# Feed-forward stages of a hybrid diffusion step: the first two pairs by plain products, weight blocks made load by load, groups placed 1-1-1-1-6

## The chip, the cores and the metric

The kernel runs on one core of one Trainium2 chip. The time is device microseconds (us) of one execution; lower is better. The engines are TensorE (PE; its weight loads are PEld), VectorE (DVE), ScalarE (ACT), GpSimd (POOL) and SyncE (SP), which here only issues DMAs.

## The reference

One step through two trunk layers for 640 tokens of 1024 features: 128 context tokens (tile 0) and 512 latent tokens (tiles 1 to 4). Layer 0 mixes with a gated MLP and a bidirectional recurrence, layer 1 with windowed attention. Each layer ends in the stage that the change is about:

```python
hp = modulate(rmsnorm(xp, norm_ffn_pre[layer]), mod_p[3], mod_p[4])
hs = modulate(rmsnorm(xs, norm_ffn_pre[layer]), mod_s[3], mod_s[4])
xp = xp + mod_p[5] * rmsnorm(sq_relu_mlp(hp, w_ffn_in[layer], w_ffn_out[layer]), norm_ffn_post[layer])
# sq_relu_mlp(h, w1, w2) = square(relu(h @ w1)) @ w2;   w1: 1024 x 4096, w2: 4096 x 1024;   xs likewise
```

Everything is in fp32. The modulation parameters (`silu(c) @ w_mod + b_mod`) of later places are computed beside other stages, 1 MB of `w_mod` at a time.

## The kernel before, in words

**Precision.** Each fp32 operand is cut into a high part (rounded to the matmul's input type by ScalarE: a "cast") and a low part (the rest: one subtraction on GpSimd or VectorE). A product of two operands is three matmuls (`split3`, L1917 to L1919): high by high, and the two mixed ones.

**Pairs.** The 4096 hidden features are worked through in 16 pairs of 2 x 128. A pair's first product is a 2 x 2 block product: weights A11, A12, A21 (its place is taken by S1), A22 of 512 features x 128 outputs each, inputs B11, B12, B21, B22 of 512 features x 320 tokens. The kernel makes it by Strassen's method in Winograd's form: 7 products P1 to P7 instead of 8, of 12 matmuls with 320 columns each. For it VectorE makes S1 to S4 of the weights in place (`adds`, L1526 to L1533) and, once per stage, T1 to T4 of the inputs (`comb`, in three slices of columns: 64, 128, 128); ScalarE casts each and GpSimd makes the low half (L1481 for the weights, L1460 for the inputs). VectorE joins the seven results (L1724 to L1733), ScalarE squares and casts them (`squared`), VectorE takes the low half (`rests`, L1541) into FH/FL.

**Groups.** The second product of a pair is 10 groups (5 token tiles x 2 output halves) of 6 matmuls with 512 columns. A group goes into one of two PSUM banks in turn; VectorE adds it to ACC (L1830) and so gives the bank back. The last two pairs are done together in G2, one step per token tile.

**Weights.** A pair's w1 and w2 are 1 MB each and are loaded by SP into RAW, which has two places: one is w1's, the other w2's. A load waits until the low halves of all blocks of the one before it in its place are made. The blocks (units of 512 columns) go to a ring of 12. For each stage an order of units is written out, and a small planner gives each unit the earliest step ("event") at which ScalarE is to cast it: after the unit 12 places before it was last used, 3 events after the last block of the load before in its place. S1 to S4 are added one event before their cast.

**Order.** All engines go through one list of steps, each in order. In the steady part pair p+1's products are interleaved with pair p's groups: P1, P6, P2, 2 groups, P5, 2 groups, P7, 2, P4, 2, P3, 2. In layer 0 the modulation of pairs 0 to 6 stands behind the second group and its transposes behind the fifth. At the head of a stage the last tiles are still being normed and transposed (`T_`, `turned_rows`, `cut`), and the order is: transposes of tile 2, P1 of pair 0, transposes of tile 3, P1 of pair 1, transposes of tile 4, P2 of pair 0, modulation, P2 of pair 1, then P6, P5, P7, P4, P3 of pair 0, then pair 1's with pair 0's groups. Before T2 and T4 overwrite X, X is stored to DRAM (`x_out`).

## Time and profile before

| | us |
|---|---|
| median of 3 runs | 1532.7 (1532.35 to 1532.74) |
| the profiled execution, its own time | 1531.43 |
| its span | 1529.6 |
| TensorE busy | 1388.7 (91%) |
| VectorE / ScalarE / GpSimd busy | 960.9 / 713.9 / 735.6 |
| mean granted TensorE clock, share of full | 0.972 |

A busy TensorE is not TensorE at its peak: matmuls overlap, so the spacing of their starts is what counts, and idle time is read from the waits. The layers' feed-forward stages are about 258 to 757 us and 1033 to 1529 us of the span.

### The profile page before, as it was taken

The numbers are of one execution on the slowest core, as the hardware profiler recorded it, in microseconds if no ns is written. First come the engines' busy times: TensorE is split into PE (matmuls) and PEld (weight loads), VectorE is DVE, ScalarE is ACT, GpSimd is POOL, SyncE is SP. The second block draws the span as 40 slices with busy tenths as digits, with TensorE's granted clock in tenths as the row PEclk, the third lists the DMA queues.
The fourth block names the chain that finished last, engine by engine and source line by source line (L and its number), as shares of the span: only waits on it lengthen the run. The fifth ranks groups of instructions, "written<-read, shape, count | busy, mean of one in ns | idle before, by whom it ended". The sixth has DMA issues, their size and how long they took to land.

```text
span 1529.6 us, 20862 instructions
## 1 busy us (share of the span) xinstructions
PE 1388.7 (91%) x7634; PEld 1163.8 (76%) x7634; DVE 960.9 (63%) x1577; ACT 713.9 (47%) x1444; POOL 735.6 (48%) x559
## 2 busy tenths in 40 slices
PE   5999997699899999999999999994899999999998
PEld 3877876577788888888867867783788888888886
DVE  5477837664466566575664588457665665766656
ACT  4467625443344344344551467555443443443443
POOL 1331413664455455455342578435564554555550
PEclk9999999799999999999999999997999999999999
DMA  9434252344543211312455100123313113122123
GB/s 351 136 109 139 84 196 82 131 157 127 184 157 111 97 69 56 110 56 83 151 192 172 55 1 2 47 64 124 138 65 128 57 56 111 56 67 99 56 83 138
DMA packets 97916, 164.33 MB, mean 107 GB/s; under 512 B 11084, under 2 KB 49688, under 8 KB 97816
## 3 DMA queue, kind: packets, MB, share of 16 engines
q1 hardware_dynamic: 86176, 157.23, 30.1%
q10 hardware_dynamic: 11640, 5.76, 1.5%
q8 instruction: 63, 1.03, 0.3%
q14 instruction: 37, 0.30, 0.1%
HBM read 154.82 MB, written 8.16 MB: 107 GB/s over the span
## 4 chain that ended last, share of the span: by engine, by line
PE 38%; DVE 4%; issue 3%; POOL 2%; ACT 2%; DMA 2%; SPq 0%; DVEq 0%; ACTq 0%; POOLq 0%
PE PS L1917 11%; PE PS L1918 10%; PE PS L1919 10%; PE PS L2253 1%; PE PS L2242 1%; PE PS L2221 1%; POOL WLU L1481 1%; DMA xd<-X 1%; PE PS L2222 1%; PE PS L1967 1%; PE PS L2205 1%; DVE X L1641 0%; DMA RAW<-in_w_ffn_in 0%; POOL GG L1428 0%; PE PS L2198 0%
## 5 line engine op out<-in xcount | busy, mean ns | idle before, releaser
L1481 POOL TENSOR_TENSOR WLU<-RAW,WHU 128x512 fp32r<-128x512 f32 x352 | 483.7, 1396 | 440.7 <-ACT WHU L1148 440.7
L1148 ACT CAST WHU<-RAW 128x512 fp32r<-128x512 f32 x352 | 204.7, 617 | 231.6 <-DMA RAW<-in_w_ffn_in 127.2
L1917 PE MATMUL PS<-WHU,MXR 128*128 128x512 f32 x640 | 257.5, 402 | 51.8 <-issue 41.5
L1830 DVE TENSOR_TENSOR ACC<-ACC,PS 128x512 f32<-128x512 f32 x260 | 175.2, 682 | 137.0 <-PE PS L1919 135.9
L1918 PE MATMUL PS<-WLU,MXR 128*128 128x512 f32 x640 | 252.4, 394 | 0.0
L1919 PE MATMUL PS<-WHU,MXR 128*128 128x512 f32 x640 | 251.6, 393 | 0.0
L1476 POOL TENSOR_TENSOR WL<-RAW,WH 128x512 fp32r<-128x512 f32 x84 | 117.5, 1430 | 213.3 <-ACT WH L1139 195.8
L1917 PEld LDWEIGHTS PS<-WHU,MXR 128*128 128x128 f32 x640 | 121.2, 189 | 90.2 <-issue 61.9
L1917 PE MATMUL PS<-HH,WHU 128*128 128x320 f32 x512 | 161.0, 314 | 20.6 <-DVE HL L1680 14.9
L1919 PE MATMUL PS<-HH,WLU 128*128 128x320 f32 x512 | 159.5, 311 | 0.0
L1918 PE MATMUL PS<-HL,WHU 128*128 128x320 f32 x512 | 159.3, 311 | 0.0
L1919 PEld LDWEIGHTS PS<-WHU,MXR 128*128 128x128 f32 x640 | 121.2, 189 | 26.8
L1918 PEld LDWEIGHTS PS<-WLU,MXR 128*128 128x128 f32 x640 | 121.4, 190 | 19.0
L1541 DVE TENSOR_TENSOR MXR<-MX,MXR 128x320 fp32r<-128x320 f32 x128 | 131.5, 1030 | 2.6 <-ACT MXR L1186 2.6
L1917 PEld LDWEIGHTS PS<-HH,WHU 128*128 128x128 f32 x512 | 97.4, 190 | 31.4 <-DVE HL L1680 15.4
L1184 ACT ACTIVATE MX<-MX 128x320 f32<-128x320 f32 x96 | 45.3, 472 | 162.5 <-DVE MX L1728 66.3
L1917 PE MATMUL PS<-WH,HH 128*128 128x512 f32 x280 | 112.6, 402 | 1.5 <-DVE ACC L1837 0.7
L1919 PE MATMUL PS<-WH,HL 128*128 128x512 f32 x280 | 109.3, 390 | 0.0
L1918 PE MATMUL PS<-WL,HH 128*128 128x512 f32 x280 | 109.1, 390 | 0.0
L1918 PEld LDWEIGHTS PS<-HL,WHU 128*128 128x128 f32 x512 | 97.4, 190 | 3.0
L1917 PE MATMUL PS<-XT,WHU 128*128 128x320 f32 x256 | 80.7, 315 | 19.9 <-POOL HFR L1460 19.9
L1919 PEld LDWEIGHTS PS<-HH,WLU 128*128 128x128 f32 x512 | 97.3, 190 | 0.0
(265 smaller groups left out, 2763.6 us busy)
## 6 DMA issues: line engine op xcount, KB each, us to landing
RAW<-in_w_ffn_in SPq DMA_DIRECT2D x32, 1024.0 KB, 6.7
RAW<-in_w_ffn_out SPq DMA_DIRECT2D x32, 1024.0 KB, 8.8
RAW<-in_w_mod SPq DMA_DIRECT2D x18, 1024.0 KB, 5.6
GG<-in_w_mod SPq DMA_DIRECT2D x13, 1024.0 KB, 9.4
MX<-in_w_mod SPq DMA_DIRECT2D x11, 1024.0 KB, 7.6
RAW<-in_w_in_even SPq DMA_DIRECT2D x7, 1024.0 KB, 5.4
RAW<-in_w_qkv SPq DMA_DIRECT2D x6, 1024.0 KB, 6.7
xd<-X SPq DMA_DIRECT2D x10, 512.0 KB, 10.3
```

The costliest lines, as they stand in the source:

```text
L1148: nc.scalar.copy(unit_view(WHU, u), unit_raw(u["ld"], u["of"])).then_inc(u_hi, 1)
L1184: link(nc.scalar.activation(z, z, ACT.Relu))
L1476: ins = nc.gpsimd.tensor_tensor(cut(ring_view(WL, ld, j)), cut(w_view(ld, b)), cut(ring_view(WH, ld, j)).bitcast(f32), ALU.subtract)
L1481: nc.gpsimd.tensor_tensor(unit_view(WLU, u), unit_raw(u["ld"], u["of"]), unit_view(WHU, u).bitcast(f32), ALU.subtract)\
L1541: V_.tensor_tensor(FL[:, slot, cols], FZ[:, slot, cols], FH[:, slot, cols].bitcast(f32), ALU.subtract).then_inc(ff_lo, 1)
L1830: V_.tensor_tensor(acc, acc, PS[:, 4 + b % 2, :], ALU.add).then_inc(b_free[b % 2], 1)
L1917: MM(out, wh, xh, start=first, stop=False, skip_group_check=reopens)
L1918: MM(out, wh, xl, start=False, stop=False, skip_group_check=reopens)
L1919: return MM(out, wl, xh, start=False, stop=last, skip_group_check=reopens)
L1967: ins = MM(PS[32 * kt:32 * kt + 32, 6 + u % 2, :], CL[:, 4 * kh + kt, :], rv[:, kt, :], start=(kh == 0), stop=(kh == 1))
L2205: ins = TR(m_bank(u)[:, P * h:P * h + P], Q2[s["n"] % 2][:, P * h:P * h + P], IDN[:, :])
L2221: MM(out, q, KH[:, g, keys], start=True, stop=False)
```

## The change

In words:
- Pairs 0 and 1 of each stage are made without the Winograd form: for each of two output blocks f and each of two column ranges (tokens 0 to 255, and 256 to 639) one step `N` of 8 x 3 matmuls, straight from the plain input. They need only A11, A12, A21, A22, so eight units and no S. ScalarE squares each result directly from its bank.
- The head's order is: transposes of tile 2, norm of tile 4, N of (pair 0, f 0, early columns), transposes of tile 3, N(0,1,early), transposes of tile 4, N(1,0,early), N(1,1,early), then the four late ones with the slices of `comb` between them, the modulation, T1 for all columns (`comb1`), and pair 0's ten groups in one run. T2 is now made from T3, and T1 is left out of the slices.
- From pair 2 on the products are Winograd's as before, with 1 group behind P6, P2, P7 and P4 and 6 behind P3; modulation behind the third group, its transposes behind the seventh.
- The order of units is now load by load (seven of w1, then four of w2); a unit may be cast 6 events (4 in the head) after the last block of the load before in its place. w2 of a pair is asked for just before w1 of the pair after the next.

```diff
@@ def ffn: order of steps
-        product(0, "P1")
-        T_(ph, TT - 2, cut=False, groups=True)
+        asked = fill[0] + (mod_load(*fill.pop(0)),)
+        w2_load(0)
         step("norm", ph=ph, t=TT - 1)
-        cut_()
+        direct(0, 0, 0)
+        T_(ph, TT - 2, groups=True)
+        direct(0, 1, 0)
+        T_(ph, TT - 1, groups=True)
+        direct(1, 0, 0)
+        direct(1, 1, 0)
         step("comb", layer=layer, c=0)
-        product(1, "P1")
+        direct(0, 0, 1)
         step("comb", layer=layer, c=1)
-        T_(ph, TT - 1, groups=True)
-        product(0, "P2")
-        mod(*fill.pop(0))
-        w2_load(0)
+        direct(0, 1, 1)
         step("comb", layer=layer, c=2)
-        product(1, "P2")
-        step("comblo", layer=layer)
-        flush()
-        for name in ("P6", "P5", "P7", "P4", "P3"):
-            product(0, name)
-        for p in range(PAIRS - 2):
+        w1_load(2)
+        direct(1, 0, 1)
+        direct(1, 1, 1)
+        mod(*asked)
+        step("comb1", layer=layer)
+        for q in range(2 * TT):
+            group(0, q)
+            if q == 4:
+                flush()
+        for p in range(1, PAIRS - 2):
             asked = fill[0] + (mod_load(*fill.pop(0)),) if fill else None
+            w2_load(p)
             w1_load(p + 2)
-            w2_load(p + 1)
             q = 0
-            for name, ngroups in ((("P6", 0), ("P5", 2), ("P7", 3), ("P4", 3), ("P3", 2)) if p == 0 else
-                                  (("P1", 0), ("P6", 0), ("P2", 2), ("P5", 2), ("P7", 2), ("P4", 2), ("P3", 2))):
+            for name, ngroups in (("P1", 0), ("P6", 1), ("P2", 1), ("P5", 0), ("P7", 1), ("P4", 1), ("P3", 6)):
...
-                    if q == 2 and asked:
+                    if q == 3 and asked:
                         mod(*asked)
-                    elif q == 5:
+                    elif q == 7:
                         flush()
@@ def ffn: order and place of the units
-        order = [(0, "A11"), (0, "A12"), (1, "A11"), (1, "A12"), (0, "S2"), (0, "S1"), (0, "A22"), (0, "S4"), (0, "S3"),
-                 (1, "S2"), (1, "S1"), (1, "A22"), (0, 0, 0), (0, 1, 0), (1, "S4"), (1, "S3"), (0, 0, 1), (0, 1, 1)]
+        order = [(p, name) for p in (0, 1) for name in ("A11", "A12", "A21", "A22")] + [(0, kt, nh) for nh in (0, 1) for kt in (0, 1)]
         for p in range(2, PAIRS):
...
-            order += [(p, "A11"), (p, "A12"), (p, "S2"), w2[0], w2[1], (p, "S1"), (p, "A22"), (p, "S4"), w2[2], w2[3], (p, "S3")]
+            order += [(p, name) for name in ("A11", "A12", "S2", "S1", "A22", "S4", "S3")]
+            if p < PAIRS - 1:
+                order += [(p - 1, kt, nh) for nh in (0, 1) for kt in (0, 1)]
...
-                    at = max(at, max(place[x] for x in place if of_load(x) == ring_order[r - 2]) + 3)
-                if o[-1] in ("S2", "S3", "S4") and o[0] > 1:
+                    freed = max(place[x] for x in place if of_load(x) == ring_order[r - 2])
+                    at = max(at, freed + (4 if freed < NS else 6))
+                if o[-1] in ("S4", "S3"):
+                    cycle = NS + 2 * TT + 17 * (o[0] - 3)
+                    at = max(at, cycle + 9 if o[0] > 2 else NS + 1)
@@ VectorE
                 elif k == "g":
                     b, acc = s["b"], ACC[:, s["t"], 512 * s["nh"]:512 * s["nh"] + 512]
                     upto(dve, b_ready, b)
+                    if not s["p"]:
+                        dve.wait_ge(t_add, 12 * s["layer"] + 12)
@@ TensorE
+                elif k == "N":
+                    layer, p, f, part = s["layer"], s["p"], s["f"], s["part"]
...
+                    if part:
+                        pe.wait_ge(n_read, DIRECTS[layer, p, f, 0])
+                    if p == 0 and f == 0:
+                        for half in (0, 1):
+                            pe.wait_ge(f_lo[half], TT * layer + (2, 5)[part])
+                    out = direct_bank(s)
+                    for i in (0, 1):
+                        u = s["units"][i]
+                        pe.wait_ge(u_lo, u["number"] + 1)
+                        wh, wl = unit_view(WHU, u), unit_view(WLU, u)
+                        for kt in range(4):
+                            xh, xl = HH[:, 4 * i + kt, DIRECT[part]], HL[:, 4 * i + kt, DIRECT[part]]
+                            ins = split3(out, (wh[:, kt, :], wl[:, kt, :]), (xh, xl), (i, kt) == (0, 0), (i, kt) == (1, 3))
+                    ins.then_inc(n_done, 1)
```

With this order, in a steady pair: A11 to A22 of pair p+2 are cast behind P1, P6, P2, the second group and P5 of pair p+1; S1 is added at P6, S2 behind the first group, S4 at P4, S3 behind the fourth group and cast behind P3; w2's four blocks are cast behind the fifth, sixth, seventh and tenth groups.

## Rows read from the trace of the kernel before

**Rows 1.** The page's first part: engine, busy us, share of the span, instructions.
```profile
PE 1388.7 (91%) x7634; PEld 1163.8 (76%) x7634; DVE 960.9 (63%) x1577; ACT 713.9 (47%) x1444; POOL 735.6 (48%) x559
```
**Rows 2.** Waits of TensorE, whole span: waiting line, releaser, total us, times, longest.
```profile
PE PS L1917 <- issue: 41.5, 28, 6.0
```
**Rows 3.** By stage: us; busy PE, PEld, DVE, ACT, POOL (count); clock; DMA share; GB/s.
```profile
258.50:338.00 79.50, 53.17 (x292) 44.82 (x293) 55.29 (x78) 40.19 (x88) 46.81 (x35) 0.83 0.43 152
338.00:720.40 382.40, 362.50 (x1994) 313.67 (x1993) 232.77 (x322) 156.86 (x314) 198.73 (x145) 0.99 0.31 102
1033.40:1112.80 79.40, 53.11 (x293) 44.71 (x294) 55.47 (x78) 40.26 (x88) 46.83 (x35) 0.83 0.36 126
1112.80:1481.10 368.30, 346.12 (x1873) 306.83 (x1872) 232.62 (x300) 156.77 (x313) 198.85 (x145) 1.00 0.24 78
```
**Rows 4.** Timeline, TensorE, head of layer 0: start, us, instruction, [idle before].
```profile
258.52 0.30 PE L2007 MATMUL PS<-IDN,ACC 128*128 128x128 f32 x1 [0.63 <-DVE ACC L1671]
267.03 0.64 PE L1917 MATMUL PS<-HH,WHU 128*128 128x320 f32 x1 [7.45 <-DVE HL L1680]
296.73 0.61 PE L1917 MATMUL PS<-XT,WHU 128*128 128x320 f32 x1 [9.87 <-POOL HFR L1460]
312.07 0.47 PE L1917 MATMUL PS<-WHU,MXR 128*128 128x512 f32 x1 [1.52 <-POOL WLU L1481]
```
**Rows 5.** Timeline, TensorE and VectorE, steady part of layer 1.
```profile
1212.15 0.69 DVE L1526 TENSOR_TENSOR RAW<-RAW 128x512 f32<-128x512 f32 x1 [3.70 <-DMA RAW<-in_w_ffn_in]
1212.76 0.68 DVE L1830 TENSOR_TENSOR ACC<-ACC,PS 128x512 f32<-128x512 f32 x1
1213.54 0.47 PE L1917 MATMUL PS<-WHU,MXR 128*128 128x512 f32 x1 [1.32 <-issue]
```
**Rows 6.** Timeline, TensorE: half a modulation step; firsts of P1, P6, two groups, P5.
```profile
317.29 1.07 PE L1967 MATMUL PS<-MX,CL 128*32 128x512 f32 x8
...
1112.79 0.30 PE L1917 MATMUL PS<-HH,WHU 128*128 128x320 f32 x1
1114.55 0.31 PE L1917 MATMUL PS<-XT,WHU 128*128 128x320 f32 x1
...
1118.07 0.39 PE L1917 MATMUL PS<-WHU,MXR 128*128 128x512 f32 x1
...
1120.81 0.30 PE L1917 MATMUL PS<-HH,WHU 128*128 128x320 f32 x1
```
**Rows 7.** Timeline, TensorE, mixer of layer 0: firsts of 24 matmuls each.
```profile
53.91 0.28 PE L1917 MATMUL PS<-HH,WH 128*128 128x256 f32 x1
...
56.79 0.34 PE L1917 MATMUL PS<-HH,WH 128*128 128x384 f32 x1
...
60.98 0.28 PE L1917 MATMUL PS<-HH,WH 128*128 128x256 f32 x1
```
**Rows 8.** Timeline, VectorE, ahead of the stage of layer 0.
```profile
253.82 1.58 DVE L1526 TENSOR_TENSOR RAW<-RAW 128x512 f32<-128x512 f32 x1
255.32 1.77 DVE L1531 TENSOR_TENSOR RAW<-RAW 128x512 f32<-128x512 f32 x1
```
**Rows 9.** Loads: a wait for X's stores, one w1 load's issue and use, w1's median (page: KB each, us to landing).
```profile
275.88 0.43 DVE L1702 TENSOR_TENSOR XTF<-ACC,EARLY_H 128x256 f32<-128x256 f32 x1 [1.83 <-DMA xd<-X]
374.97 0.37 SPq L1092 DMA_DIRECT2D RAW<-in_w_ffn_in  x1
388.17 0.62 ACT L1148 CAST WHU<-RAW 128x512 fp32r<-128x512 f32 x1 [11.05 <-DMA RAW<-in_w_ffn_in]
RAW<-in_w_ffn_in SPq DMA_DIRECT2D x32, 1024.0 KB, 6.7
```
**Rows 10.** Groups by line: VectorE from 1184 to 1436 us, and GpSimd's cut (page): count, busy us, mean ns.
```profile
L1541 DVE TENSOR_TENSOR MXR<-MX,MXR 128x320 fp32r<-128x320 f32 x36 | 43.1, 1197 | 0.0
L1533 DVE TENSOR_TENSOR RAW<-RAW 128x512 f32<-128x512 f32 x18 | 22.2, 1235 | 0.0
L1481 POOL TENSOR_TENSOR WLU<-RAW,WHU 128x512 fp32r<-128x512 f32 x352 | 483.7, 1396 | 440.7 <-ACT WHU L1148 440.7
```

More of the change, by code:

```diff
@@ L257, in ffn, with holder @@
                         for nh in (0, 1):
-                            used[p, kt, nh] = e
-        place, before = {}, -2
-        ring_order = [x for p in range(PAIRS) for x in ([("w1", p)] + ([("w2", p - 1)] if p else []))] + [("w2", PAIRS - 1)]
+                            uses((p, kt, nh), e)
+        def holder(k):
+            return k - UNITS + (2 if k < 2 * UNITS - 2 else 0)
+        place, before = {}, -3
         ring_order = [("w1", 0), ("w1", 1)] + [x for p in range(PAIRS - 2) for x in (("w2", p), ("w1", p + 2))] + \
@@ L297, in ffn @@
                     steps[events[e + late]].setdefault("rest", []).append((s["p"], s["name"]))
+            elif s["kind"] == "N":
+                s["units"] = [by_name[layer, s["p"], f"A{s['f'] + 1}{k}"] for k in (1, 2)]
+                steps[events[e + 1]].setdefault("rest", []).append((s["p"], (s["f"], s["part"])))
             elif s["kind"] == "g":
@@ L841, in hybrid_step @@
         GROUP_B = {(s["layer"], s["p"]): s["b"] for s in STEPS if s["kind"] == "g"}
-        RESTS = {(s["layer"], s["p"], s["name"]): k + 1 for k, s in
-                 enumerate(s for s in STEPS if s["kind"] == "P" and s["name"] in OUTPUT)}
+        RESTS = {}
+        for s in STEPS:
+            if s["kind"] == "N" or s["kind"] == "P" and s["name"] in OUTPUT:
+                RESTS[s["layer"], s["p"], s["name"] if s["kind"] == "P" else (s["f"], s["part"])] = len(RESTS) + 1
         TURNS = {(s["ph"], s["t"]): s for s in STEPS if s["kind"] == "T"}
@@ L953, in ring_view @@
             return buf[:, j % RING, :]
+        DIRECTS = {(s["layer"], s["p"], s["f"], s["part"]): i + 1 for i, s in enumerate(s for s in STEPS if s["kind"] == "N")}
         BLOCK_LOAD = {}
@@ L1022, in out_cols, with bank_of, direct_bank, outputs_done @@
             return slice(HALF * late, HALF * late + HALF)
-        def bank_of(name, p):
-            b = {"P1": 2 if p == 1 else 0, "P2": 2 if p == 1 else 0, "P6": 1, "P7": 1, "P5": 2, "P3": 2, "P4": 3}[name]
-            return PS[:, b, 0:HALF]
+        def bank_of(name):
+            return PS[:, {"P1": 0, "P2": 0, "P6": 1, "P7": 1, "P5": 2, "P3": 2, "P4": 3}[name], 0:HALF]
+        DIRECT = (slice(0, 2 * P), slice(2 * P, TOK))
+        NP = PAIRS - 2
+        def direct_bank(s):
+            cols = DIRECT[s["part"]]
+            return PS[:, 2 * s["p"] + s["f"], 0:cols.stop - cols.start]
+        def outputs_done(layer, p, t):
+            return RESTS[layer, p, ("P4" if t < 2 else "P3") if p > 1 else (1, int(t > 1))]
+        def output(slot, name):
+            if name in OUTPUT:
+                f, late = OUTPUT[name]
+                return slot + f, out_cols(late)
+            return slot + name[0], DIRECT[name[1]]
         def modc(layer, c):
@@ L1720, in _ @@
                         dve.wait_ge(p_done, s["count"] + 1)
[L1721 removed]
+                        bank = bank_of(name)
                     if name == "P6":
```

202 lines of the change are left out of this document (102 added, 100 removed).

## The prediction

> **What bounds the kernel now.** I read the page's busy times first: TensorE is busy for 91% of the span, no other engine for more than 63% [rows 1]. So time can only be won where TensorE stands still or does work that can be left out. The list of its waits says where: 41.5 us in 28 waits are put down to "issue" [rows 2], none of them to a named engine. The busy table by stage then splits each feed-forward stage in two [rows 3]. In the head (from the transposes of tile 2 to the first product of pair 2; 79.5 and 79.4 us) TensorE is busy for 53 us only and its mean clock is 0.83; in the rest up to the first product of pair 15 (382.4 and 368.3 us) it is busy 94 to 95%.
>
> The head's timeline shows the holes [rows 4]: 7.45 us before the first product (it needs the low half of tile 2), 9.87 us before P6 (it needs T2 of all columns), 1.52 us before the first second-matrix group (its block's low half is late). Between them products and transposes wait for one another, and after a hole the granted clock is at the lower of its two levels (1.2 of 2.4 GHz) for a while, hence the mean of 0.83 [rows 3].
>
> In the steady part one hole comes back in each pair: 1.32 us before the matmul at 1213.54. The profile calls it "issue", but VectorE's rows at the same moment name it [rows 5]: VectorE stood 3.70 us in front of S1 (L1526), waiting for the load of w1, and the accumulation of a group (L1830, 1212.76 to 1213.44) is queued behind it. TensorE waits for that bank and goes on 0.1 us after it ends. The accumulation itself was due long before.
>
> **Prices.** A product (12 matmuls of 320 columns) takes 1114.55-1112.79 = 1.76 us, two groups (12 matmuls of 512 columns) 1120.81-1118.07 = 2.74 us, so 1.37 each [rows 6]. A pair without holes is 7 x 1.76 + 10 x 1.37 = 26.0 us. The 13 pairs between the bounds of the steady part [rows 3] would be 338.0 us. Layer 1 takes 368.3 [rows 3], 30.3 more, 2.3 per pair; layer 0 382.4, of which six modulation steps are 13.3, leaving 31.1: a step is 16 matmuls of which eight last 1.07 us [rows 6], so 1.9 with overlap, and four transposes, 0.3; 2.2 in all.
>
> **Part 1, plain products in place of the first two pairs.** Each pair now has four results (two output blocks by 256 and 384 columns) of 24 matmuls each. The same shapes stand in an earlier stage: 24 of 256 columns take 56.79-53.91 = 2.88 us, 24 of 384 take 60.98-56.79 = 4.19 [rows 7]. Four and four are 28.3 us, against 14 products at 1.76 = 24.6: TensorE has 3.7 us more work per layer. What goes for it:
> - Nothing in the first four results needs tiles 2 to 4. They need tiles 0 and 1, both halves of the features. Tile 1's low half stood behind two additions on VectorE (1.58 and 1.77 us [rows 8]) that pairs 0 and 1 no longer need; without them it ends at about 258.4, and the first result starts at about 259, right behind the transposes of tile 2, which start at 258.52 [rows 4]. The 7.45 us go.
> - The four early results (11.5 us) lie beside the norm, transposes and cuts of tiles 3 and 4. Tile 4's transposes must wait until VectorE has read tile 3's bank: I count about 1 us of waiting there. Tile 4's low half is there at about 273, when the four have ended: 0.3 us.
> - The four late ones (16.8 us, about 273.5 to 290) lie beside the three T2, T3, T4 combinations, which therefore stop nothing; the 9.87 us and the wait ahead of them go. T1 shares its place with the plain input, so it comes behind the last plain result, but its first user (P5 of pair 2) is over 15 us later.
> - The second-matrix blocks of pair 0 are cut beside them, so the 1.52 us go.
>
> TensorE's own sum for the head is then 0.8 (transposes of tile 2) + 28.3 + 1.6 (two more tiles' transposes) + 2.2 (modulation) + 13.7 (ten groups) = 46.7 us. VectorE becomes the second limit: of the 55 us it had here [rows 3] I take off 14 of combinations, low halves and additions of pairs 0 and 1 and add 3 for low halves of tiles 3 and 4: some 44 us, with gaps. In order on it stand the modulation copy, the three T1 additions (about 3 us) and only then the first copies out of the groups' two banks, then S4 and S3 of pair 2. ScalarE has a wait of its own: the casts of w2 of pair 0 stand behind the third plain result (at about 272), and that load comes behind five 512 KB stores of X, whose wait ended at 275.88 in the profile [rows 9]; ScalarE will stand until about 278 with the squares behind it, and VectorE's low halves wait for those. I put 9 us on the sum for all this: 55.5 us in place of 79.45. Its bounds are 49 (the waits of 1 and 0.3 and 1 at the groups) and 68 (the store's landing and T1's chain both in full, 6 and 8 us, and the lower clock behind them for 4). Gain 24 us per layer, 48 in all.
>
> The first modulation after the head falls one pair later, so one of them (2.2 us) moves from each head into the steady part.
>
> **Part 2, blocks load by load, and groups 1-1-1-1-6.** Before, w1's last block (S3) and w2's last blocks were cut together, and the next w1 was asked for only then, 6.7 us (the page's median to landing [rows 9]) ahead of VectorE's first need. Now w1's seven blocks come first. I count in one pair from the start of P1: P4 ends at 14.7, P3 at 17.8, six groups end at 26.0, and the next P1 and P6 at 29.5. S3 is cast behind P3's squares, its low half ends at about 22.3; 6.7 us later, at 29.0, w1 is there, and VectorE comes to S1 behind P6, at 30.1. So nothing waits, and what would be late next has room: behind S1 stands only the accumulation of one group, whose bank TensorE needs again 6.6 us later, since P2, a group, P5 and P7 lie between. Even the longest landing that I found (asked for at 374.97, used at 388.17, 13.2 us [rows 9]) would not quite reach it. The w2 load is asked for at about 28 and first needed at 47. In layer 0 the two modulation loads go out just ahead of w2 at about 15 and the three land by 25 to 28; w2's casts are due at 22 and the groups that use them at 31.7: covered.
>
> What can be late is VectorE in the six groups. From the end of P4 (t = 0) it has c21 0.5, S4, the low half of P7, one accumulation 0.7, S3, c12 0.5, the low half of P4, and then the accumulation of group 4. TensorE needs that bank at 5.9. A low half takes 1.20 on average and an addition like S3 1.24 [rows 10]; the accumulation (L1830) reads PSUM and is not changed by its neighbours. With these means: 0.5+1.2+1.2+0.7+1.2+0.5+1.2+0.7 = 7.2, late by 1.3. With the short values (0.7 for the additions, 0.5 for the low halves) 4.8, not late. GpSimd has nothing to cut during the first half of that stretch, so I take a value between: 1.0 us per pair, from 0 to 3.
>
> The Trainium skill ("SBUF — State Buffer", section "Who interferes with whom") says that a VectorE instruction with two SBUF inputs and a GpSimd instruction that reads SBUF exclude each other for a whole instruction. The trace agrees: L1541 (two inputs in SBUF) has a mean of 1.20 us [rows 10], and the accumulation, which reads one input from PSUM, takes 0.68 [rows 5]. Rival D is what the rule would do at its worst.
>
> So a steady pair is 27.0 us. Layer 0: 13 x 27.0 + 7 x 2.2 = 366.4, against 382.4, 16.0 less. Layer 1: 351.0 + 2.2 = 353.2 against 368.3, 15.1 less. The tail behind pair 15's first product keeps its order and its wait, and I leave it at nothing, as everything outside the feed-forward stages: its instructions don't change.
>
> **Sum.** 48 + 16 + 15 = 79 us off the profiled execution's 1531.4 us (span 1529.6): 1452.4. The median of the runs is 1.3 us above that execution, so I forecast 1454 us.
>
> **Rivals.**
> - A, TensorE's floor: the head at 51 and a pair at 26.2 us. For it: in the trace TensorE keeps 26.0 whenever nobody holds it. Heads 57 less, steady part 26 + 26 less: 1422. 12%.
> - B, the six groups stall on VectorE: 3.0 us per pair, the four two-input operations at the length that they have beside GpSimd (1.5 to 1.7, as the additions of [rows 8]). Against it: GpSimd is busy for half of the time only. That is 26 x 2.0 = 52 us more than forecast: 1506. Half of that (2.0 per pair): 1480. Together 20%.
> - C, the head gives back: w2's late load and T1's chain leave it at 68 us. 2 x 12.5 more: 1479. 8%.
> - D, slower than before: the six-group run again, but with each of the four two-input operations first waiting for a whole cut of GpSimd (mean 1.40 [rows 10]) and then running (0.5 to 0.7), and GpSimd's cuts delayed by them in turn, so that the next pair's blocks are late too. It decides from 79/26 = 3.0 us per pair above my 1.0, so from 4.0; at 4.5 the time is 1454 + 26 x 3.5 = 1545. In full that is 4 x 2.0 + 2.4 = 10.4 (four of them lie ahead of the bank) against 5.9 available, 4.5 late. Against it: GpSimd has some two cuts in that stretch, not four. 4%.
> - E, the holes have another cause (instruction supply, as "issue" could be read) and stay, and the head's are eaten by the added products: about no change, 1532. The 0.1 us between accumulation and restart [rows 5] speaks against it. 2%.
> The forecast has the remaining 54%, with a range of its own of 1438 to 1470. For 8 in 10 the range takes in part of A, C and half of B: 1430 to 1488. A change of 0.2% is about what a measurement of this kernel can tell: faster 94%, within 0.2% 2%, slower 4%.
>
> **What would show it.** The head of each layer (transposes of tile 2 to P1 of pair 2) at 52 to 60 us, with a granted clock near 1 and no wait of TensorE over 2 us until the groups. In the steady part 26.2 to 28 us per pair, no VectorE wait for w1 with an accumulation due behind it, and what is left of waiting inside the last six groups, behind accumulations. Wrong would be: a head over 65 us, a wait of TensorE for a combination or a block's low half in pair 2, or pairs at 28 us and more.

## The result and the profile after

The changed kernel takes 1441.1 us (median of 4 runs, 1440.0 to 1441.7) against 1532.7 us: ratio 0.940, 95% interval 0.9385 to 0.9417, so 92 us less. The forecast was 1454 (1430 to 1488). The profiled execution has a span of 1439.6 us, 90.0 less than before.

The page's first part, as in [rows 1], and TensorE's waits, as in [rows 2]:

```profile
PE 1373.5 (95%) x7682; PEld 1163.8 (81%) x7682; DVE 853.0 (59%) x1541; ACT 705.3 (49%) x1428; POOL 718.3 (50%) x547
```

```profile
PE PS L1970 <- issue: 17.1, 4, 8.3
```

The table by stage, with the same bounds and columns as [rows 3] (transposes of tile 2, first product of pair 2, first product of pair 15, in layer 0 and in layer 1):

```profile
258.80:320.60 61.80, 50.81 (x297) 45.08 (x296) 48.05 (x60) 34.71 (x77) 42.90 (x30) 0.92 0.51 179
320.60:676.80 356.20, 356.20 (x2014) 311.43 (x2013) 191.08 (x325) 156.30 (x313) 194.62 (x144) 1.00 0.35 116
988.74:1051.20 62.46, 51.12 (x297) 45.23 (x296) 48.11 (x60) 34.68 (x77) 42.92 (x30) 0.92 0.50 177
1051.20:1392.50 341.30, 341.22 (x1894) 306.85 (x1894) 184.42 (x303) 155.66 (x313) 195.96 (x144) 1.00 0.26 84
```

In the steady part nothing is left to win by removing waits: TensorE is busy in all of it, at the full clock. The heads still have waits. Against [rows 3] the heads give 17.6 and 16.8 us, the steady parts 26.3 and 27.0, and the tail 1.4 (48.5 to 47.1; its wait before P2 is gone); the sum is 89.1, and most of the rest of the 90.0 lies between the stages (from the first product of pair 15 of layer 0 to the head of layer 1, 313.1 to 311.9).

The 26.3 us of layer 0's steady part don't come evenly from its 13 pairs. One of them (pair 3, from its first product to pair 4's) took 37.3 us and now takes 28.6. In the kernel before, VectorE stood there 10.41 us for w1 and TensorE 5.97 us behind it (timelines):

```profile
388.18 0.69 DVE L1526 TENSOR_TENSOR RAW<-RAW 128x512 f32<-128x512 f32 x1 [10.41 <-DMA RAW<-in_w_ffn_in]
389.57 0.76 PE L1917 MATMUL PS<-WHU,MXR 128*128 128x512 f32 x1 [5.97 <-issue]
```

This is the load of [rows 9] that landed 13.2 us after it was asked for. It was asked for 3.5 us behind a store of the new state (4 KB), which ScalarE issues together with three other transfers (two of 256 KB, one of 4 KB). In the kernel after, the w1 load nearest to that store goes out 6.3 us ahead of it and lands in 5.4 us. The 14 traces of this case divide in this way: the w1 load nearest to the store lands in 5.4 to 5.7 us where it is asked for ahead of it (nine traces), and in 11.7 to 15.2 us where it is asked for 0.4 to 3.5 us behind it (five). No run separates the four transfers. So 8.7 us of layer 0's gain go with the place of one load.

TensorE in the head of layer 0 (timeline; start, duration, instruction, wait before it), the answer to [rows 4]:

```profile
258.81 1.04 PE L2060 MATMUL PS<-IDN,ACC 128*128 128x128 f32 x8
...
267.65 0.63 PE L2060 MATMUL PS<-IDN,ACC 128*128 128x128 f32 x4 [1.06 <-DVE ACC L1730]
269.87 1.12 PE L2060 MATMUL PS<-IDN,ACC 128*128 128x128 f32 x4 [1.59 <-ACT ACC L1213]
...
306.87 0.77 PE L1970 MATMUL PS<-WHU,MXR 128*128 128x512 f32 x1 [7.87 <-issue]
...
316.48 0.47 PE L1970 MATMUL PS<-WHU,MXR 128*128 128x512 f32 x1 [0.47 <-issue]
```

The 7.45, 9.87 and 1.52 us of [rows 4] are gone. In their place stands one hole of 7.87 us ahead of the third group (8.29 in layer 1). As in [rows 5], the word "issue" hides a bank that VectorE has not read yet. In the kernel before this holds for every one of the 28 waits of [rows 2]: each ends 0.10 us after VectorE's accumulation or copy out of a bank has ended. Behind a wait for w1 stood 22 of these, behind a wait for GpSimd's cut four, and the other two are in the heads. VectorE at that moment, and what ScalarE waited for earlier (timelines):

```profile
296.43 1.70 DVE L1591 TENSOR_TENSOR RAW<-RAW 128x512 f32<-128x512 f32 x1 [1.25 <-POOL WLU L1541]
298.05 3.18 DVE L1600 TENSOR_TENSOR MXR<-MX,MXR 128x384 fp32r<-128x384 f32 x2
301.16 0.68 DVE L1645 COPY PART<-PS 128x512 f32<-128x512 f32 x1
301.76 4.21 DVE L1764 TENSOR_TENSOR EARLY_H<-ACC 128x256 f32<-128x256 f32 x3
306.07 0.69 DVE L1885 COPY ACC<-PS 128x512 f32<-128x512 f32 x1
```

```profile
279.87 1.14 ACT L1202 CAST WHU<-RAW 128x512 fp32r<-128x512 f32 x2 [3.22 <-DMA RAW<-in_w_ffn_out]
```

Read upwards from the copy (L1885) that frees the first group's bank: three T1 additions (L1764), the modulation copy (L1645), two low halves of plain results (L1600), S2 (L1591). Groups 1 and 2 had filled both banks by 299.0; TensorE goes on 0.11 us after the copy ends.

In the steady part of layer 1, VectorE around the last six groups of a pair:

```profile
1173.14 0.49 DVE L1781 TENSOR_TENSOR MX<-PS,MX 128x320 f32<-128x320 f32 x1 [1.06 <-PE PS L1972]
1173.55 0.68 DVE L1593 TENSOR_TENSOR RAW<-RAW 128x512 f32<-128x512 f32 x1
1174.15 0.48 DVE L1600 TENSOR_TENSOR MXR<-MX,MXR 128x320 fp32r<-128x320 f32 x1
1174.55 0.68 DVE L1883 TENSOR_TENSOR ACC<-ACC,PS 128x512 f32<-128x512 f32 x1
1175.15 0.68 DVE L1593 TENSOR_TENSOR RAW<-RAW 128x512 f32<-128x512 f32 x1
1176.29 0.49 DVE L1784 TENSOR_TENSOR MX<-PS,MX 128x320 f32<-128x320 f32 x1 [0.45 <-PE PS L1972]
1176.69 0.68 DVE L1600 TENSOR_TENSOR MXR<-MX,MXR 128x320 fp32r<-128x320 f32 x1
1177.67 0.69 DVE L1883 TENSOR_TENSOR ACC<-ACC,PS 128x512 f32<-128x512 f32 x1 [0.29 <-PE PS L1972]
```

These are the very operations that the forecast summed. VectorE waits for TensorE among them (1.06, 0.45, 0.29), not the other way round. GpSimd's cuts (timeline) leave a gap of 4.50 us there, from 1171.24 to 1175.74:

```profile
1167.13 4.11 POOL L1541 TENSOR_TENSOR WLU<-RAW,WHU 128x512 fp32r<-128x512 f32 x3 [2.90 <-ACT WHU L1202]
1175.74 1.29 POOL L1541 TENSOR_TENSOR WLU<-RAW,WHU 128x512 fp32r<-128x512 f32 x1 [4.50 <-ACT WHU L1202]
```

### The profile page after: what moved, and what is told of

The parts are those of the page before. It is cut to its first block and busy times, and to the rows that moved or that the text cites. A ratio compares the mean times of both kernels' runs of the same rounds, so it can differ in the third digit from the quotient of the medians.

```text
span 1439.6 us, 20860 instructions
## 1 busy us (share of the span) xinstructions
PE 1373.5 (95%) x7682; PEld 1163.8 (81%) x7682; DVE 853.0 (59%) x1541; ACT 705.3 (49%) x1428; POOL 718.3 (50%) x547
## 5 line engine op out<-in xcount | busy, mean ns | idle before, releaser
L1541 POOL TENSOR_TENSOR WLU<-RAW,WHU 128x512 fp32r<-128x512 f32 x340 | 460.5, 1378 | 371.2 <-ACT WHU L1202 371.2
L1202 ACT CAST WHU<-RAW 128x512 fp32r<-128x512 f32 x340 | 195.7, 618 | 161.4 <-PE PS L1972 117.8
L1970 PE MATMUL PS<-WHU,MXR 128*128 128x512 f32 x640 | 253.6, 396 | 19.4 <-issue 17.1
L1970 PE MATMUL PS<-HH,WHU 128*128 128x320 f32 (+2 forms) x576 | 178.9, 311 | 0.0
L1972 PE MATMUL PS<-HH,WLU 128*128 128x320 f32 (+2 forms) x576 | 178.7, 310 | 0.0
L1971 PE MATMUL PS<-HL,WHU 128*128 128x320 f32 (+2 forms) x576 | 178.7, 310 | 0.0
L1972 PEld LDWEIGHTS PS<-WHU,MXR 128*128 128x128 f32 x640 | 121.0, 189 | 26.6
L1970 PEld LDWEIGHTS PS<-HH,WHU 128*128 128x128 f32 x576 | 109.5, 190 | 4.9 <-issue 0.2
L1971 PEld LDWEIGHTS PS<-HL,WHU 128*128 128x128 f32 x576 | 109.4, 190 | 4.3
L1972 PEld LDWEIGHTS PS<-HH,WLU 128*128 128x128 f32 x576 | 109.3, 190 | 0.0
L1600 DVE TENSOR_TENSOR MXR<-MX,MXR 128x320 fp32r<-128x320 f32 (+2 forms) x128 | 89.3, 702 | 8.5 <-ACT MXR L1322 7.2
L1970 PE MATMUL PS<-XT,WHU 128*128 128x320 f32 x224 | 70.0, 312 | 0.0
```

What stands on the lines that cost most here:

```text
L1202: nc.scalar.copy(unit_view(WHU, u), unit_raw(u["ld"], u["of"])).then_inc(u_hi, 1)
L1541: nc.gpsimd.tensor_tensor(unit_view(WLU, u), unit_raw(u["ld"], u["of"]), unit_view(WHU, u).bitcast(f32), ALU.subtract)\
L1600: V_.tensor_tensor(FL[:, slot, cols], FZ[:, slot, cols], FH[:, slot, cols].bitcast(f32), ALU.subtract).then_inc(ff_lo, 1)
L1970: MM(out, wh, xh, start=first, stop=False, skip_group_check=reopens)
L1971: MM(out, wh, xl, start=False, stop=False, skip_group_check=reopens)
L1972: return MM(out, wl, xh, start=False, stop=last, skip_group_check=reopens)
```

## The experiments

Stages in us (layer 0 / layer 1), all from profiled executions with the bounds of [rows 3]; "late pair" is the distance between first products of later pairs of layer 1; "won" is one less the ratio to before, times 1532.7, with its interval. The kernels are told of one by one below.

```
                 heads          steady parts     late pair   won
before           79.5 / 79.3    382.4 / 368.3    28.0         -
after            61.9 / 62.5    356.1 / 341.2    26.03       91.8 (89.4 to 94.3)
b_both           78.7 / 80.6    363.2 / 350.3    26.03       43.1 (40.2 to 45.8)
b_units_new      78.9 / 78.4    368.0 / 352.8    26.6        34.0 (31.6 to 36.5)
b_groups_new     80.0 / 79.5    375.5 / 361.6    27.3        15.5 (12.4 to 18.4)
b_s1_later       80.5 / 79.4    380.0 / 371.6    28.2         0.5 (-2.6 to 3.7)
a_head_only      62.4 / 62.0    378.2 / 366.0    28.1        43.4 (40.3 to 46.6)
after_again      64.0 / 63.2    356.1 / 341.2    26.03       93.0 (90.7 to 95.2)
a_w2_later       61.0 / 60.7    356.1 / 341.3    26.03       97.2 (94.1 to 100.1)
a_s12_later      58.6 / 58.1    356.8 / 342.5    26.03       99.5 (96.9 to 102.1)
a_both           57.8 / 56.7    356.7 / 342.5    26.03      103.6 (100.7 to 106.5)
a_t1_between     57.0 / 57.4    358.9 / 343.7    26.03       98.6 (96.1 to 100.9)
a_t1_early       59.5 / 58.7    358.0 / 343.5    26.03       97.2 (94.4 to 99.9)
a_pool_twice     61.6 / 62.4    356.7 / 341.2    26.03       93.0 (90.3 to 95.9)
```

### The steady part alone, in whole and in halves

The kernel before with this edit to the groups (b_groups_new), this to the order of the blocks (b_units_new), and both (b_both; there S1 is also added behind A12, as in the kernel after):

```diff
-    (("P1", 0), ("P6", 0), ("P2", 2), ("P5", 2), ("P7", 2), ("P4", 2), ("P3", 2))
+    (("P1", 0), ("P6", 1), ("P2", 1), ("P5", 0), ("P7", 1), ("P4", 1), ("P3", 6))
```

```diff
-            order += [(p, "A11"), (p, "A12"), (p, "S2"), w2[0], w2[1], (p, "S1"), (p, "A22"), (p, "S4"), w2[2], w2[3], (p, "S3")]
+            order += [(p, name) for name in ("A11", "A12", "S2", "S1", "A22", "S4", "S3")]
+            if p < PAIRS - 1:
+                order += [(p - 1, kt, nh) for nh in (0, 1) for kt in (0, 1)]
```

> The kernel before with the steady part of the change alone: blocks made load by load (w1's seven, then w2's four) and groups behind the products 1-1-1-1-6; both heads as before, the first two pairs of each stage in seven products. Theory (the trace of after read by stages): the steady part gives 53 us of the 92, the head 35 to 39, and the two do not touch each other: about 1478 us (1474 to 1483), and no TensorE start more than 0.5 us late in the steady part. Rival (the forecast's own split, head 48, steady part 31): 1501 us. Second rival: the steady part is clean only because the new head hands over an early schedule; then under 20 us are gained here, over 1512 us.

> The kernel before with one edit: a pair's blocks are made load by load (w1's seven first, then w2's four), so the next w1 is asked for as soon as S3 is cast. The groups stay where they were (none behind P6, two behind P2, P5, P7, P4, P3 and so on) and the heads too. Theory: the hole per pair is VectorE's wait for w1 ahead of S1 with an accumulation queued behind it; asking earlier takes it away by itself, and what is left is nothing: 1478 to 1485 us. Rival (the order of the groups does the work, because an accumulation must not be due close behind S1): 1510 to 1533 us, little gained. Rival (the hole is instruction supply at a fixed place in the code): 1530 us.

> The kernel before with one edit: the ten groups of a pair lie 1-1-1-1-6 behind P6, P2, P7, P4 and the last product P3, none elsewhere. The blocks are still made with w1's and w2's mixed, so w1 is asked for as late as before. Theory: VectorE still stands before S1 until w1 lands, but now with one accumulation behind it and not two, and the six groups at the end end later: between 10 and 30 us gained, 1503 to 1523 us. Rival (the groups are what the change is worth in the steady part): 1478 to 1485 us. Rival (six groups in a row stall on VectorE, the forecast's case B): 1540 us and more.

Measured: 1489.5, 1499.3 and 1517.4 us. A late pair falls from 28.0 to 27.3 by the groups, to 26.6 by the blocks and to 26.03 by both: 0.7 and 1.4 make 2.0, so in the settled pairs the two parts nearly add. The groups came out inside the theory's 1503 to 1523; the other two missed theirs by some 6 and 14 us at the slow end. Against TensorE's own time (26.03 us a pair, 28.57 with a modulation) the steady parts of b_units_new are 29 us too long. Some 10 of these are 0.6 us in each of the 17 late pairs, in which TensorE still waits 0.2 to 0.8 us for an accumulation that stands behind S2, and S2 behind GpSimd's cut. Another 8 are pair 3 of layer 0, which takes 36.8 us: its w1 was asked for 0.4 us behind the store and landed in 15.2 us, and TensorE stood 6.27 us. The rest lies in the first pairs. What b_both lacks is in its pair 2: from P1 of pair 2 to P1 of pair 3 it takes 35.5 and 38.0 us, against 28.6 and 28.9 in the kernel after. There TensorE waits in layer 1 (timeline) for a low half and behind VectorE, whose S4 had stood 3.38 us for GpSimd:

```profile
1100.88 0.47 PE L1920 MATMUL PS<-WHU,MXR 128*128 128x512 f32 x1 [3.48 <-POOL WLU L1484]
```

```profile
1120.41 1.66 DVE L1536 TENSOR_TENSOR RAW<-RAW 128x512 f32<-128x512 f32 x1 [3.38 <-POOL WLU L1484]
```

The old head hands its blocks over too late for the new order; one pair later that is over. So the second rival (clean only because of the new head) fails: 37 us of the steady part's 53 come without it, and the other 16 are the two pairs 2 (6.9 + 9.1).

### One addition moved in VectorE's queue

```diff
+                if o[-1] == "S2" and o[0] > 2:
+                    at = max(at, place[o[0], "A12"] + 2)
...
-            elif o[-1] == "A11":
+            elif o[-1] == ("A11" if o[0] < 3 else "A12"):
                 steps[index(place[o])].setdefault("add", []).append(dict(layer=layer, ld=u["ld"], of=(o[0], "S1")))
```

S1 of pairs 3 and later moves one step back, and S2 stays behind it.

> The kernel before with one addition moved on VectorE: from pair 3 on, S1 = A11+A12 stands one step later in its queue, behind A12's cut instead of behind A11's, and S2 behind that; loads, products and groups are as before, and so w1 lands as late as before. Theory (the hole is VectorE's queue: it stands for w1 in front of S1 with the accumulation that TensorE needs queued behind): the accumulation now goes ahead of the wait, and most of the 1.3 to 1.7 us per pair goes: 26 x 1.5 = 39, about 1494 us (1485 to 1505). Rival (instruction supply or whatever else the word issue covers): the time stays at 1533 us within 2. Rival (the late blocks themselves would stop TensorE next): under 15 us gained, and a wait of a product for its block in the profile.

Measured: 1532.6 us, nothing won. That is the rival's time, but not its mechanism. VectorE and TensorE in one pair (timelines):

```profile
1212.10 0.69 DVE L1528 TENSOR_TENSOR RAW<-RAW 128x512 f32<-128x512 f32 x1 [2.31 <-DMA RAW<-in_w_ffn_in]
1212.71 0.49 DVE L1543 TENSOR_TENSOR MXR<-MX,MXR 128x320 fp32r<-128x320 f32 x1
1214.44 1.69 DVE L1533 TENSOR_TENSOR RAW<-RAW 128x512 f32<-128x512 f32 x1 [1.25 <-POOL WLU L1483]
1216.06 1.27 DVE L1832 TENSOR_TENSOR ACC<-ACC,PS 128x512 f32<-128x512 f32 x2
```

```profile
1216.84 0.47 PE L1919 MATMUL PS<-WHU,MXR 128*128 128x512 f32 x1 [1.51 <-issue]
```

The wait for w1 now has no accumulation behind it, and the hole has left its place between the groups behind P5: it stands behind P7. But S2, which comes next, waits 1.25 us for GpSimd's cut and takes 1.69 us beside the next one, and two accumulations are behind that. TensorE starts 0.1 us after the first of them ends, as in [rows 5]. So my theory was right about the queue and wrong about the price: with w1 as late as before, what is made from it is late, and taking one waiting instruction out of the queue brings the next one to its front. Fixed code as the cause is refuted by the hole's move.

The same is seen from the other side in b_units_new, where VectorE still stands 3.00 us for w1 ahead of S1, but early enough for the accumulation behind it (timeline):

```profile
1244.43 0.69 DVE L1527 TENSOR_TENSOR RAW<-RAW 128x512 f32<-128x512 f32 x1 [3.00 <-DMA RAW<-in_w_ffn_in]
1245.04 0.68 DVE L1831 TENSOR_TENSOR ACC<-ACC,PS 128x512 f32<-128x512 f32 x1
```

### The head alone

The kernel before with the new head (first two pairs by plain products, in the order of the kernel after); from pair 2 on blocks and groups as before.

```diff
-            for name, ngroups in (("P1", 0), ("P6", 1), ("P2", 1), ("P5", 0), ("P7", 1), ("P4", 1), ("P3", 6)):
+            for name, ngroups in (("P1", 0), ("P6", 0), ("P2", 2), ("P5", 2), ("P7", 2), ("P4", 2), ("P3", 2)):
```

(shown against the kernel after; the order of the blocks goes back as well.)

> The kernel before with the head of the change alone: pairs 0 and 1 of each stage by plain products, in the order of the kernel after; from pair 2 on blocks mixed and groups placed as before. Theory: the head gives 35 to 40 us here as in the kernel after, and the steady part keeps its holes: 1533 - 37 = 1496 us (1490 to 1502). Rival (the forecast's sizes): 48 us, 1485 us. Rival (the two parts need each other; in the old order the head's lateness on VectorE and in the loads is carried on through the pairs): 1505 us or more.

Measured: 1491.7 us, 43.4 won (40.3 to 46.6), more than the 35 to 40 expected. The heads account for 17.1 and 17.3; another 4.2 and 2.3 lie in the first pairs of the old steady part, and its holes stay (28.1 per pair). In layer 0 the late w1 only changes its pair: 37.5 us in pair 4, with TensorE standing 6.76 us. The two parts alone make 86.5 of the whole's 91.8. The missing 5 are about what the three intervals allow. The stages show that the new order loses 10 us where it meets the old head, in b_both's pairs 2 (35.5 and 38.0, before 32.2 and 31.4), and that the new head helps the old order's first pairs.

### What makes the hole in the new head

Edits to the kernel after. a_w2_later: w2's casts of pair 0 on ScalarE one plain result later. a_s12_later: S1 and S2 of pair 2 behind T1 in VectorE's queue. a_both: both.

```diff
+                if k == 8:
+                    at = 3
+                if o == (2, "S2"):
+                    at = NS + 3
...
-                steps[index(place[o])].setdefault("add", []).append(dict(layer=layer, ld=u["ld"], of=(o[0], "S1")))
+                steps[index(place[o] if o[0] > 2 else NS + 1)].setdefault("add", []).append(dict(layer=layer, ld=u["ld"], of=(o[0], "S1")))
```

> The kernel after with ScalarE's casts of w2 of pair 0 one plain result later in each layer, so that ScalarE does not stand before them for the load while squares that VectorE needs are queued behind. Theory (the hole of 8 us between the second and third group is VectorE's queue in the head, and ScalarE's stand for the load at 276.7 to 279.9 is the first 3 us of it): 2 x 3 = 6 us less, 1435 us (1433 to 1438), and the hole at about 5 us. Rival (VectorE's own queue is full from the end of the second plain result on, and the stand only takes what would be waited for later): 1441 within 1. Rival (w2's cut now ends too late and its first group waits): 1443 us or more.

> The kernel after with the additions S1 and S2 of pair 2 moved on VectorE from ahead of the T1 additions to behind them (their first user, P1's neighbours of pair 2, comes after all ten groups). Theory: TensorE's hole of 8 us is VectorE's queue ahead of the first copy out of a group's bank; two additions (some 1.2 to 1.5 us each) less in it shorten the hole by 2.5 to 3 us per layer; the groups' run has room for them: 1435 to 1437 us. Rival (they come back as a wait between groups or of S4's product): 1441 within 1, with a smaller hole and a new one behind it.

> Both edits to the kernel after: w2's casts of pair 0 one result later, and S1, S2 of pair 2 behind T1. Theory: the two shorten the same queue and add: hole about 2 us in place of 8, 1441 - 12 = 1429 us (1428 to 1433), and more of the head at the full clock. Rival (the queue is bound by GpSimd's or ScalarE's chain once two pieces are out): 1434 to 1437 us. Rival (given back at P1 or P2 of pair 2): 1439 to 1441 us.

In a_w2_later only the first two lines (`k == 8`) are changed, in a_s12_later only the others.

Measured: 1437.6, 1435.7 and 1431.9 us. TensorE ahead of the third group of layer 0 in the three (timelines), against 7.87 in the kernel after:

```profile
304.74 0.77 PE L1972 MATMUL PS<-WHU,MXR 128*128 128x512 f32 x1 [6.94 <-issue]
```

```profile
303.75 0.47 PE L1972 MATMUL PS<-WHU,MXR 128*128 128x512 f32 x1 [4.44 <-issue]
```

```profile
302.69 0.47 PE L1974 MATMUL PS<-WHU,MXR 128*128 128x512 f32 x1 [3.56 <-issue]
```

S1 and S2 behave as the theory says: the hole is 3.4 us shorter (4.3 in layer 1, 8.29 to 3.95), with 0.6 and 1.2 us given back in the first steady pair. ScalarE's stand is worth less than I thought, 0.9 and 1.3 us of hole and not 3: VectorE's queue has more in front than what ScalarE delays. Its time fell inside the expected 1433 to 1438 us all the same, but the stages show only 2.6 us of it in the two heads, and its interval (0.9347 to 0.9386) overlaps that of the kernel after when measured again, so of this edit alone no gain is shown. The same kernel's heads differ by 2.2 and 0.7 us between two executions (after and after_again), and single holes by 1.0 us. The two edits shorten the same queue and nearly add (5.4 and 7.7 us by the ratios, 11.8 together). a_both is the fastest kernel here: its interval, 0.9305 to 0.9343 of before, lies below both of the kernel after's, 0.9385 to 0.9417 and 0.9379 to 0.9408 (after_again).

### T1 between the copies

T1's additions read only the half of the rows that the five groups with nh=0 overwrite. a_t1_between takes pair 0's groups with nh=1 first, puts one T1 addition behind each of the first three copies and S1, S2 behind the fourth (with w2's casts later, as above). a_t1_early puts S1 and S2 behind the third copy, and the small gate operations three groups later.

```diff
-            step("g", uses_b=1, layer=layer, p=p, nh=q // TT, t=q % TT)
+            step("g", uses_b=1, layer=layer, p=p, nh=q // TT if p else 1 - q // TT, t=q % TT)
...
-        step("comb1", layer=layer)
         for q in range(2 * TT):
             group(0, q)
+            for c in (0, 1, 2):
+                if q == (0, 1, 2)[c]:
+                    step("comb1", layer=layer, c=c)
...
-                        dve.wait_ge(t_add, 12 * s["layer"] + 12)
+                        dve.wait_ge(t_add, 12 * s["layer"] + (9 if s["nh"] else 12))
```

> The kernel after, unchanged, as the control for the edits to its head, in one set of runs with the next two. Both theories: 1441 us within 2, the hole between its second and third group at 7 to 8.5 us in both layers, 26.03 us per pair in the steady part of layer 1.

> The kernel after with w2's casts of pair 0 one result later, and with the T1 additions no longer ahead of the groups: pair 0's five groups of the output's second half come first (T1 reads the first half of the rows that a group's first copy overwrites, and only that), and T1's three additions lie between their copies, one behind each of the first three; S1, S2 of pair 2 behind the fourth. Theory (the hole is the 4.9 us of T1's additions, queued on VectorE ahead of the first copy out of a bank): no wait over 1.5 us at the groups, head at 55 to 57 us, 1425 us (1421 to 1430). Rival (VectorE is full all through the groups, since its additions take 1 to 1.6 us beside GpSimd's cuts and the copies 0.7, against 1.37 per group): the wait is only spread over groups three to seven, the head stays at 58 us, as with S1 and S2 alone moved: 1430 to 1434 us. Rival (given back, because T1's and w2's blocks of pair 1 come later and stop pair 2): 1436 us or more.

> The kernel a_t1_between (T1's three additions between the first group copies) with two things put back or moved: S1, S2 of pair 2 and all blocks behind them one step earlier (as in a_both), and the small gate operations of VectorE, which took 3.3 us between two copies there, three groups later. Theory (in a_t1_between the 5 us won in each head came back in part as 2.3 us at the gate operations and 2.4 us in pair 2's groups, both from VectorE's queue): both go for the most part, heads 55 to 56 us, pair 2 at 26.5 us (layer 1 with modulation 29), 1426 us (1422 to 1430), below both kernels and below a_both. Rival (VectorE is simply full through the ten groups, whatever the order): the same 57 us and 1431 to 1436 us. Rival (its queue is now worse ahead of the fourth copy): a wait of 2 us and more there, 1434 us or more.

Measured: 1441.5, 1435.8 and 1437.5 us. The hole of 7.9 us is gone in both (0.61 us in its place in layer 0, 1.41 and 1.32 in layer 1). Both kernels also have the two edits before, which had left 3.56 and 2.85 us of it. So moving T1 took away the last 3.0 and 1.5 us. S1 and S2 alone had taken 3.4 and 4.3 us, ScalarE's stand alone 0.9 and 1.3. The hole is the sum of what stands in the queue and has no single cause. But a smaller hole comes later. In a_t1_between it is 2.32 us behind two gate operations of VectorE on 128x8 elements, in a_t1_early 3.76 us behind S3, ahead of the tenth group. VectorE and GpSimd in a_t1_between, then VectorE in a_t1_early (timelines):

```profile
305.14 2.10 DVE L1665 TENSOR_TENSOR GC<-GC,GCB 128x8 f32<-128x8 f32 x1
307.28 1.19 DVE L1666 TENSOR_TENSOR GC<-GC,GCN 128x8 f32<-128x8 f32 x1
308.39 1.27 DVE L1891 COPY ACC<-PS 128x512 f32<-128x512 f32 x2
```

```profile
303.86 3.36 POOL L1527 TENSOR_TENSOR HL<-EARLY_H,HH 128x1280 fp32r<-128x1280 f32 x1 [3.13 <-ACT HH L1320]
307.18 5.46 POOL L1547 TENSOR_TENSOR WLU<-RAW,WHU 128x512 fp32r<-128x512 f32 x4
```

```profile
313.28 1.66 DVE L1599 TENSOR_TENSOR RAW<-RAW 128x512 f32<-128x512 f32 x1 [3.12 <-POOL WLU L1547]
...
315.68 0.17 DVE L1665 TENSOR_TENSOR GC<-GC,GCB 128x8 f32<-128x8 f32 x1
```

The first gate operation took 2.10 us, until GpSimd's T1 low half ended (303.86 + 3.36 = 307.22). Moved away from it, it takes 0.17 us again, but S3's addition waits 3.12 us for GpSimd's cuts, which stand behind that same T1 low half in GpSimd's queue (306.06 to 309.02 there). So neither theory was right: VectorE is not full, and the order did not cure it; the chain through GpSimd is next. Pair 2 also gives back time: in layer 1 31.35 us against 28.92. I had put that down to the blocks' coming a step later, but in a_t1_early, where they are back in their place, it still takes 31.12, and its cause stays open. Both times lie some 11 us above the theories, by the rivals in which the gain is given back. a_both, with no edit to T1, stays ahead of both, by 4 and 6 us.

### GpSimd's work doubled in the steady part

```diff
                     pool.wait_ge(u_hi, u["number"] + 1)
+                    if len(u["of"]) == 2 and u["of"][0] > 2 and u["of"][1] in ("S1", "A22", "S4", "S3"):
+                        again[0] += 1
+                        nc.gpsimd.tensor_tensor(unit_view(WLU, u), unit_raw(u["ld"], u["of"]), unit_view(WHU, u).bitcast(f32), ALU.subtract).then_inc(twice, 1)
+                        pool.wait_ge(twice, again[0])
```

> The kernel after, in which GpSimd makes the low halves of S1, A22, S4 and S3 twice in every pair from 3 on (the same values; some 5 us more of GpSimd per pair, in the stretch in which VectorE has its S4, S3 and low halves to make ahead of the six groups' accumulations). Theory (the steady part keeps TensorE's own 26.03 us per pair because GpSimd stands still in that stretch, so that VectorE's two-input operations take 0.5 to 0.7 us and not the 1.2 that the forecast reckoned with): their mean rises to 1.0 us and more, TensorE waits inside the six groups, 26.5 to 28 us per pair, 1455 to 1490 us. Rival (VectorE has room there in any case, and the forecast's order of the accumulations was wrong): VectorE's operations get longer and the pair stays at 26.03 to 26.2 us, 1441 to 1446 us. Rival (GpSimd itself becomes late): the pair is over 28 us, and the products wait for their block's low half.

Measured: 1441.6 us, as after_again, and 26.03 us per pair. VectorE in the steady part of layer 1, 1130 to 1360 us, grouped by line (count, busy us, mean ns, idle before), first in the kernel after (S3 and S4, S2, S1), then in this one (S3 and S4, S1, S2):

```profile
L1593 DVE TENSOR_TENSOR RAW<-RAW 128x512 f32<-128x512 f32 x18 | 12.3, 683 | 0.0
L1591 DVE TENSOR_TENSOR RAW<-RAW 128x512 f32<-128x512 f32 x9 | 7.5, 828 | 0.0
L1586 DVE TENSOR_TENSOR RAW<-RAW 128x512 f32<-128x512 f32 x9 | 6.3, 704 | 0.0
```

```profile
L1598 DVE TENSOR_TENSOR RAW<-RAW 128x512 f32<-128x512 f32 x18 | 15.0, 834 | 0.0
L1591 DVE TENSOR_TENSOR RAW<-RAW 128x512 f32<-128x512 f32 x9 | 12.0, 1336 | 0.0
L1596 DVE TENSOR_TENSOR RAW<-RAW 128x512 f32<-128x512 f32 x9 | 10.7, 1185 | 0.0
```

The operations get longer (S1 0.70 to 1.34 us) and TensorE does not notice, so the rival holds for this much of a burden, and VectorE had room. The theory is only half tested, though. In the stretch between P4 and P3 GpSimd still waited 1.74 us for ScalarE's cast (in the pair at 1172 us), and S3 and S4 rose to 0.83 only, not to the 1.24 of [rows 10]. Whether the pair would hold with all four operations at 1.2 us stays open.

## Why the prediction was right, and where its sizes were not

- **What bounds the kernel, and where the time can be won**: right. Of the 90 us of span only 15 are TensorE's busy time (1388.7 to 1373.5, the lower clock's share with it); the rest is time in which it stood.
- **The hole per pair is VectorE's queue in front of w1**: right, and gone. The experiments sharpen it: it needs w1 early, not only another order behind it. The forecast's 2.3 us per pair are an average, though: a late pair lost 2.0 (28.0 against 26.03), and pair 3 of layer 0 alone 8.7. It took the landing of 13.2 us as the longest that may come, not as the loss of one known pair.
- **Steady pair, 27.0 us**: too slow; 26.03 is TensorE's own sum of 26.0. The failed term is the 1.0 us per pair for VectorE in the six groups, worked out from the means of [rows 10]. Those means belong to the old schedule, in which VectorE's work lay beside GpSimd's cuts. In the new one the low halves have a mean of 0.63 us, and the chain of 4.8 us, which the forecast also wrote down, is the one that came. 26 pairs by 0.97 are 25 us too many.
- **A modulation step, 2.2 us**: too low. A pair with one takes 28.57 us in layer 0, one without 26.03, so 2.5; layer 1's only one costs 2.9 (28.92). For eight of them that is 3 us too few. The forecast had six in layer 0 before and seven after, and that was so. Steady parts in all: 22 us better than forecast.
- **The head, 55.5 us**: too fast; 61.9 and 62.5. TensorE's sum of 46.7 holds. The 9 us put on it should have been 15: waits of 1.06, 1.59, 7.87 and 0.47 us (11.0) and the lower clock (an estimate: 0.08 of 50.8 busy us, 4.1). Each piece was named: tile 4's transposes (1.3 forecast, 2.65), T1's chain ahead of the first copy (3 us forecast for the additions, 4.21), ScalarE's stand for w2 (until 278 forecast, 279.87 measured). VectorE's total was nearly right (some 44 forecast, 48.05 measured). What failed is the step from total to hole: these pieces lie one behind the other in a single in-order queue in front of one copy, and I added only part of each. Heads in all: 13 us worse than forecast.
- **The tail at nothing**: it gave 1.4 us.
- **Sum**: 22 better, 13 worse, 1.4 and 0.8 better elsewhere: 11 us better than the forecast's span. Two errors of opposite sign made the total look better than its parts.
- **Rivals**: A (floor) came true in the steady part; C (the head gives back, 68 us) came halfway; B and D did not occur: GpSimd's cuts lie elsewhere, and with four more of them per pair (a_pool_twice) the pair still took 26.03 us; E is refuted by the 28 waits that all end 0.10 us after VectorE, by the holes that went and by the one that moved.

The statements on what the profile would show: no wait over 2 us ahead of the groups, held (1.59); the clock near 1, not quite (0.92, lower around the two stops); the head in 52 to 60 us, missed by 2 and 2.5; the pair in 26.2 to 28, missed at the good end; what is left of waiting inside the last six groups, wrong, there is none.

## What to carry to other kernels

An in-order queue is priced by what stands in front of the instruction that somebody waits for, not by the engine's total: list that queue, and sum it. A wait that the profile calls "issue" is worth a look at the engine that empties the bank; if its instruction ends 0.1 us before the restart, that is the cause. Moving one instruction behind a late load helps little when its successors need the same load; ask for the load earlier. And durations taken under one schedule don't carry over to another when two engines get in each other's way: take the short and the long value, and look where the neighbour's work will lie.

## What the runs showed of the hardware

A VectorE operation with two inputs in SBUF, however small, can last until the GpSimd instruction beside it ends: 128x8 elements took 0.17 us in one kernel, and in another 2.10 us, until 0.02 us after the end of a GpSimd subtraction of 3.36 us that had begun before it. The copy and the accumulation, which read PSUM, kept their 0.68 us in every schedule.

The price can be told exactly. In the kernel before, 92 of VectorE's weight additions (128x512) begin while a GpSimd subtraction runs, and every one ends 0.55 us after that subtraction does (0.545 to 0.557). With no GpSimd subtraction beside it such an addition takes 0.68 us. The low halves (128x320) end 0.35 us after it. The S2 of the head shown above is one: it lasted until 298.13, and GpSimd's cut until 297.58 (timeline of the kernel after):

```profile
294.60 2.98 POOL L1541 TENSOR_TENSOR WLU<-RAW,WHU 128x512 fp32r<-128x512 f32 x2
```

So a delay is what is left of the GpSimd instruction at that moment, and not a slower rate. It goes the other way too: a cut of GpSimd takes 1.30 us (median), and 1.55 when it begins while a two-input VectorE operation runs, at most 1.76. The Trainium skill ("SBUF — State Buffer", section "Who interferes with whom") says that a VectorE instruction with two SBUF inputs contends with a GpSimd instruction that reads SBUF, through a port pair that is an exclusive lock. These rows agree: the operation that began second waits for the first.

Doubling four of GpSimd's cuts per pair left the mean of its cuts as it was (1.39 us in the kernel after, 1.37 and 1.39 in that one) and made VectorE's S1 0.63 us longer. The share of its cuts that begin beside a two-input VectorE operation stayed at a third (113 of 340, and 146 of 444), while more of VectorE's additions met a running GpSimd subtraction (56 of 112, and 75 of 112).

The w1 load of 1 MB nearest to ScalarE's four transfers took 5.4 to 5.7 us to land when it was asked for ahead of the store of the new state, and 11.7 to 15.2 us when it was asked for just behind it (nine and five traces). Which of the four delays it, no run shows.
